# Attention on a ring of four score banks, with ScalarE's high half ahead of exponentials and VectorE's low half ahead of maxima

## The reference, cut to what matters

```python
for window, dilation in DILATED_PATTERNS:          # (128, 1), (512, 4), (2048, 16)
    o_i, lse_i = dilated_window_attn(q, k, v, window, dilation)
mix_w = jax.nn.softmax(jnp.stack(lses, axis=0), axis=0)
o = jnp.sum(mix_w[..., None] * jnp.stack(outs, axis=0), axis=0)
attn_out = o.reshape(B, S, ATTN_WIDTH) * jax.nn.silu(g_attn)
```

## Time and profile before

| what | value |
|---|---|
| profiled execution, its own time | 2792.35 us |
| its span | 2790.5 us |
| attention in the span | 401.6 to 625.4 us |
| busy in the whole span: TensorE, VectorE, ScalarE | 2565.1, 1328.6, 1183.5 us |
| mean granted TensorE clock | 0.966 of full |

### The profile page before, as it was taken

How to read it: one execution, slowest core, us unless ns; L and a number is a source line. 1 busy time by engine, 2 the same in 40 slices (tenths; PEclk the granted TensorE clock), 3 DMA queues, 4 the chain that set the end, 5 groups by cost and what they waited for, 6 DMA issues and landing times. The chain is left out here.

```text
span 2790.5 us, 30843 instructions
## 1 busy us (share of the span) xinstructions
PE 2565.1 (92%) x12104; PEld 2082.2 (75%) x12104; DVE 1328.6 (48%) x1716; ACT 1183.5 (42%) x1709; POOL 634.0 (23%) x520
## 2 busy tenths in 40 slices
PE   7999988879999999999998879999985999999992
PEld 6888866668787888878887668785774888888881
DVE  5530217764213212145424643105126888888885
ACT  4212227763241212123323522334213877777772
POOL 2312303323221313141301542354101111111100
PEclk9999999999999999999998989999986999999996
DMA  5433145523310131142215522441344999999995
GB/s 177 151 117 106 46 103 134 134 61 130 104 61 31 46 121 61 61 109 82 91 61 181 166 98 83 140 154 61 131 161 161 381 380 377 381 377 378 372 367 197
DMA packets 168690, 455.78 MB, mean 163 GB/s; under 512 B 17920, under 2 KB 85664, under 8 KB 155872
## 3 DMA queue, kind: packets, MB, share of 16 engines
q1 hardware_dynamic: 117856, 384.98, 38.3%
q10 hardware_dynamic: 37760, 41.17, 4.3%
q0 software_dynamic: 12928, 27.63, 2.8%
HBM read 389.23 MB, written 82.31 MB: 169 GB/s over the span
## 5 line engine op out<-in xcount | busy, mean ns | idle before, releaser
L2673 DVE TENSOR_TENSOR ex_w_lo<-ex_w,ex_w_hi 128x2048 fp32r<-128x2048 f32 x198 | 448.1, 2290 | 83.6 <-ACT ex_w_hi L2618 81.8
L2618 ACT ACTIVATE ex_w_hi<-ex_w 128x2048 fp32r<-128x2048 f32 x198 | 378.9, 1915 | 53.3 <-PEq L2219 26.4
L219 POOL TENSOR_TENSOR p_w_lo<-w_raw,p_w_hi 128x512 fp32r<-128x512 f32 (+1 forms) x154 | 203.3, 1352 | 632.2 <-ACT p_w_hi L239 607.2
L219 POOL TENSOR_TENSOR p_w_lo_rest<-w_raw,p_w_hi_rest 128x512 fp32r<-128x512 f32 x94 | 125.3, 1367 | 254.0 <-ACT p_w_hi_rest L239 254.0
L264 PE MATMUL o_ps<-o_w_hi,o_m_hi 128*128 128x512 f32 x384 | 154.6, 403 | 11.0 <-DVE split_cols L1175 11.0
L266 PE MATMUL o_ps<-o_w_hi,split_cols 128*128 128x512 f32 x384 | 152.9, 398 | 0.0
L265 PE MATMUL o_ps<-o_w_lo,o_m_hi 128*128 128x512 f32 x384 | 152.8, 398 | 0.0
L264 PE MATMUL p_ps<-p_w_hi,hT_hi 128*128 128x512 f32 (+1 forms) x320 | 120.8, 378 | 0.0
L266 PE MATMUL p_ps<-p_w_hi,hT_lo 128*128 128x512 f32 (+1 forms) x320 | 118.5, 370 | 0.0
L2485 POOL DMA_INDIRECT ex_x<-xn_rows,slot_token x33 | 36.1, 1093 | 362.0 <-PE ex_px L2532 327.0
L265 PE MATMUL p_ps<-p_w_lo,hT_hi 128*128 128x512 f32 (+1 forms) x320 | 118.1, 369 | 0.0
(11 more groups left out here) (475 smaller groups left out, 6463.0 us busy)
## 6 DMA issues: line engine op xcount, KB each, us to landing
ex_w<-w SPq DMA_DIRECT2D x99, 2048.0 KB, 13.9
w_raw<-w_in SPq DMA_DIRECT2D x42, 1024.0 KB, 5.1
x_rows<-o_x SPq DMA_DIRECT2D x24, 512.0 KB, 2.6
att_k<-k_columns SPq DMA_DIRECT2D x46, 256.0 KB, 7.6
w_raw<-w_out SPq DMA_DIRECT2D x8, 1024.0 KB, 9.6
qk_columns<-qk_y ACTq DMA_DIRECT2D x16, 512.0 KB, 2.6
o_x<-x_rows SPq DMA_DIRECT2D x16, 512.0 KB, 3.7
w_raw<-w_xkv SPq DMA_DIRECT2D x8, 1024.0 KB, 6.0
```

The lines of the kernel that those rows point to most:

```text
L219: emit(self.lo(n)[:, 0:w], self.half(n // (KC // 2), w)[:, n % (KC // 2), :], self.hi(n)[:, 0:w].bitcast(F32), ALU.subtract).then_inc(self ...
L2618: nc.scalar.activation(w_hi[:, n % RING, :], raw_half(n), ACT.Copy).then_inc(hi_done, 1)
L2673: nc.vector.tensor_tensor(w_lo[:, n % RING, :], raw_half(n), w_hi[:, n % RING, :].bitcast(F32), ALU.subtract).then_inc(down_lo if m == "w2 ...
```

## The change

Three things, all inside `attention`.

- The scores' PSUM is no longer two buffers of two banks, taken in turn by row. It is four banks: rows 0 to 3 take banks 0 to 3, one each; rows 4 and 6 take banks 0 and 1, rows 5 and 7 banks 2 and 3. S of row a waits for M of the row that used its banks last: 2, 3, 3, 4, 3, 2, 2, 2 rows before, for a = 0 to 7. It was 2 for all.
- VectorE issues L of the last block ahead of M of the row at hand, where it was behind it.
- ScalarE issues K of a block (and the copy of the sums) ahead of E of the row before it, where it was behind.

```diff
-        ps_s = s.enter_context(nc.psum_tensor("att_ps_s", [P, 2, S], F32))
+        ps_s = s.enter_context(nc.psum_tensor("att_ps_s", [P, 4 * BANK], F32))
...
+        def score_banks(i):
+            a = row(i)[1]
+            at = (a if a < HALF else 2 * (a % 2)) * BANK
+            return ps_s[:, at:at + (a + 1) * P]
+
+        def freed_scores(engine, i):
+            a = row(i)[1]
+            last = i - (2, 3, 3, 4, 3, 2, 2, 2)[a]
+            if last >= 0:
+                engine.wait_ge(maxed, last + 1)
...
-                    if i >= 2:
-                        pe.wait_ge(maxed, i - 1)
+                    freed_scores(pe, i)
+                    banks = score_banks(i)
...
                 for kind, n in items():                 # VectorE
+                    if late is not None:
+                        take_lo(late)
                     if kind == "row":
                         maxes(n)
-                    if late is not None:
-                        take_lo(late)
                     late = n if kind == "block" and n < BLOCKS else None
...
                 for kind, n in items():                 # ScalarE
-                    if late is not None:
-                        exps(late)
-                    late = n if kind == "row" else None
                     if kind == "sums":
                         keep_scales(n)
                     if kind == "block" and n < BLOCKS:
                         keep_hi(n)
+                    if late is not None:
+                        exps(late)
+                    late = n if kind == "row" else None
```

More of the change, by code:

```diff
@@ L829, in scores @@
                         for part in range(2):
-                            ins = pe.matmul(ps_s[:, i % 2, u:u + m], qs[:, h % 2, a * P:(a + 1) * P],
+                            ins = pe.matmul(banks[:, u:u + m], qs[:, h % 2, a * P:(a + 1) * P],
                                             ks[:, h % 2, part, u:u + m], start=(part == 0), stop=(part == 1))
@@ L894, in maxes @@
                         dve.wait_ge(turned, turns_of_blocks(12 * (h - 1) + (FIRST_BLOCKS if a < HALF else 12)))
-                    nc.vector.tensor_tensor_reduce(x, ps_s[:, i % 2, 0:n], logc[:, S - n:S], -SCALE, -NEG, ALU.add,
+                    nc.vector.tensor_tensor_reduce(x, score_banks(i), logc[:, S - n:S], -SCALE, -NEG, ALU.add,
                                                    ALU.min, nmx[:, i:i + 1]).then_inc(maxed, 1)
```

## The result

Six runs of the changed kernel took 2796.49 to 2803.85 us, median 2802.12. The kernel before, run in turn with it, took 2790.42 in the median (six runs). The ratio is 1.0040, 95% interval 1.0028 to 1.0052: slower by 11.7 us, about twice the 0.2% that such a measurement can tell from nothing.

A forecast was written before the change was run, and what follows sets the result against it. No engine was full; the chain of block turns, high halves and low halves set the pace. First halves +11.5, second halves -6.2 gave +5.3, at most 7.7; 6.5 taken on 2792.05 gave 2798.5 us, range 2789.5 to 2805.

The forecast's parts named there:

- first halves, odd heads, x5: Row 5's scores to block 4's turn, behind a half without sums: from 7.52 to 8.34 or 8.35 us, +0.83 each.
- first halves, even heads, x5: Row 5's scores to block 4's turn, behind a half with sums: from 7.40 to 8.45 us, +1.05 each.
- second halves with sums, x5: Block 4's turn to the next head's row 5 scores, with two sums: 11.44 us, gain 0.81 each, 4.05 together.
- second half of head 0; of even heads 2 to 10, x5: Block 4's turn to next head's row 5 scores, without sums: 8.96 us, gain 0.36 each, 2.16 over six.
- The chain of the first half: Row 5's maximum waits behind block 0's low half, delaying later scores, copies, exponentials; block 4's turn 8.34 us after row 5's scores.
- E7: Row 7's exponentials on ScalarE: start 7.06 us after row 5's scores; block 4's turn waits for them, 1.28 later.
- The unknown: ScalarE's low copy directly behind exponentials: if they cannot overlap, 0.11 us more per half, 22 halves, +2.4; otherwise nothing.
- E6: Row 6's exponentials on ScalarE, ahead of the low copy in the first half: counted as 1.04 us.
- Rival 1: Attention: first halves spared, second halves' gain stands; -6.2 us, 2785.9; chance 0.12.
- Rival 2: Attention: first halves lose half of what was counted, cancelling the second halves' gain; -0.5 us, 2791.6; chance 0.20.
- Rival 4: Score banks: they can't run ahead, as TensorE issues one row ahead; costs nothing, part of the forecast, no separate chance.
- Rival 3: TensorE inside heads: new waits make the granted clock fall, 0.8 us in each of 11 heads, +9, 2807; chance 0.13.

The follow-up runs named there:

- ring_scalar: Changed kernel with VectorE's order put back, keeping the four score banks and ScalarE's swap; median 2794.72 us, ratio 1.0012 to the kernel before.
- ring_only: Changed kernel with VectorE's and ScalarE's orders both put back, keeping only the four score banks; median 2794.78 us, ratio 1.0013 to the kernel before.
- scalar_only: Kernel before with ScalarE's swap alone: two score buffers in turn and VectorE's order as before; median 2794.99 us, ratio 1.0015.
- s3_early: ring_scalar with the next head's row 3 scores issued right behind its row 2 scores on TensorE; median 2786.29 us, ratio 0.9981 to the kernel before.
- two_swaps: Changed kernel with two score buffers taken in turn instead of four banks, both engines' swaps kept; median 2807.60 us, ratio 1.0060 to the kernel before.

## Why the prediction was right, and where its sum was short

The forecast was a slower kernel, by 5.3 to 7.7 with 6.5 taken, through a longer first half and a shorter second. That is what happened; the size was nearly twice. The median, 2802.12, lies in the range of 2789.5 to 2805 but above the 2796 to 2801 of the forecast itself, and the kernel before was 1.6 faster in these runs than in the three that the forecast started from (2790.42 against 2792.05), which by luck brings the time nearer to the forecast than the change is. One of the prediction's own signs of being wrong came as well: the granted clock left 1.00 inside attention, once, at a cost of 0.9. Term by term, from the two profiles (where a term stands for five heads, their mean):

| term | predicted | measured |
|---|---|---|
| first half of head 0 | +1.0 | +1.6 |
| first halves, odd heads, x5 | +0.83 each | 8.53 - 7.51 = +1.02 |
| first halves, even heads, x5 | +1.05 each | from 7.40 to 8.64, +1.25 |
| first half of head 11 | +1.08 | 8.53 - 7.26 = +1.27 |
| second halves with sums, x5 | -0.81 each | from 12.25 to 11.76, -0.50 |
| second half of head 0; of even heads 2 to 10, x5 | -0.36 each | -0.40; 9.17 - 9.32 = -0.15 |
| clock, fall in head 9 | 0 | +0.9 |
| clock, last head's pause | 0 | -0.8 |
| sum | +5.3 | +10.7 |

**The chain of the first half held link by link.** Predicted and measured from S5: M5 2.56 and 2.57, S7 3.57 and 3.58, T2 4.54 and 4.61, M7 5.71 and 5.79, E7 7.06 and 7.25, T4 8.35 and 8.53. M0, which ended the half before, is no longer what T4 waits for.

**The unknown lay at its upper end.** The low copy does not overlap the exponential ahead of it: E6 at 505.55, its read over at 506.68, the copy at 506.70. That is 1.15 where I had 1.04, and 0.11 in each of 22 halves is 2.4. I had stated both ends and taken the middle, though the nearest row, the low copy behind K2, already pointed to the upper one.

**A step was left out: the add.** The low copy now lies behind E2, so VectorE's add waits for it, and L7 is queued behind the add. In the second half with sums (VectorE; M3 follows):

```profile
515.01 0.69 DVE L931 TENSOR_TENSOR att_tot<-att_ps_o,att_low 64x512 f32<-64x512 f32 x1 [0.52 <-ACT att_low L976]
515.74 0.69 DVE L923 TENSOR_TENSOR att_pT_lo<-att_ps_t,att_pT_hi 128x512 fp32r<-128x512 f32 x1
```

K7 started at 515.01, so L7 could have gone at 515.62 or so; behind the add it went at 515.74. That is 0.12, in the five second halves with sums: 0.6. (In those without sums the add is over before L7 is ready.) T9 is 7.72 after T4, not 7.45; the other 0.15 of this lag are the low copy's 0.11, counted above, and small steps.

**A row from another setting.** S7 to T2 was taken as 0.97 from a row in which TensorE came straight from other work. Behind a pause S7's matmuls take 1.20 and T2 comes 1.03 after. With head 0 at +1.6 instead of +1.0 this is another 1.3. The three together, 2.4 + 0.6 + 1.3, lift 5.3 to 9.6. Of the last 1.1, the clock's net is 0.1, and some 0.9 are the sum of small steps in the ten regular second halves, each 0.1 longer than I added them up; no single one stands out.

**Which swap does what.** From the halves of ring_scalar without falls, ScalarE's swap (with the ring, which alone leaves the pair as it was) changes a pair by +0.28, -0.52, +0.08 and -0.60, together -0.76. VectorE's swap on top then adds +0.95, +0.37, +0.93 and +0.10, together +2.4. The prediction worked both out at once and so took the second halves' gain as common; it is ScalarE's alone, and VectorE's swap costs in all four halves.

**The rivals.** Rival 1 needed M5 within 1.6 of S5; it came at 2.57. Rival 2 needed a first half that loses half of what I counted; it lost more. Rival 4 is right of the ring alone, and off by 0.3 a pair in the changed kernel. Rival 3, the clock: the changed kernel has waits of 0.74, 0.72 and 0.85 in each first half, as worked out, and fell once in ten heads:

```profile
586.00:588.00 2.00, 2.00 (x14) 1.88 (x15) 1.18 (x2) 1.35 (x4) 0.00 (x0) 0.50 1.02 221
```

That fall cost 0.86 (12.63 for its half against 11.77). The rival priced it well, 0.8, but had it in eleven heads, where it came in one. It described other kernels of this study: those with one pause of 1.6 ahead of T4 lost the clock in five and seven heads of ten. By the rule of the Trainium skill ("TensorE: Matmul & The Clock Gate", section "A second HAM failure mode: psum-queue depth-cycling"), short pauses between groups of matmuls would have done it in the changed kernel; its trace disagrees in nine heads of ten, and ring_scalar's agrees in five.

Not settled: where ring_only's untraced runs lose the 4 that its stage doesn't show, and whether the changed kernel's untraced runs, all 3 to 7 longer than the profiled one, had more falls. Their mean clock was 0.965 to 0.966 against its 0.968, which would fit and shows no place.

## What to carry to other kernels

When work is moved ahead of other work on one in-order engine, follow everything queued behind it to the next engine and back; here one low half ahead of one maximum delayed the next scores, the next exponentials and the next transposes in turn. The instruction to put first was the one that the longest waiter needed (E7 for T4), and not the one whose class waited most in total. And a pause of TensorE is priced with what comes behind it: a saving that leaves one long pause can be taken back by the clock, so look at the granted clock behind each pause before trusting a sum of durations.

## What the runs showed of the hardware that I had not expected

- A pause of 1.64 ahead of T4, once per head of 18, was enough for a granted clock of 0.50 in five of ten heads (ring_scalar), and the same pause did not bring a fall every time. The longest pause alone does not sort the kernels: 1.26 to 1.40 in each head brought six falls (scalar_only), 1.2 in each head four (s3_early), nothing over 0.96 two (two_swaps), 0.7 to 0.86 three times a head one (changed); 0.9 and 1.2 in odd heads with 1.0 in even ones brought none (before), and neither did 1.0 and 1.4 with 1.1 (ring_only, traced execution).
- Six added matmuls of 512 columns, 1.55 in each of eleven heads, made ring_scalar 5.8 faster.
- An exponential lets another exponential or a high copy of 128 partitions start about 0.1 before its accumulator is read out (E6 491.83 - 490.81 = 1.02 to E7, reads included, against 1.15 to the low copy, which takes 64 partitions from one half of the partitions to the other).
